# Attention-to-sampling hand-over of a hybrid decoder step: order of the absorption's transpositions, two-half weight return, later sigmoids, gate products in the last head pair

## The reference, cut to what matters

```python
o_a = _prompt_attention(q, keys, vals) * jax.nn.silu(z_a)        # 16 heads of 64, blocks of 128 queries
...
q_lat = jnp.einsum('bthd,rhd->bthr', q[..., :QK_NOPE] * g_k[:QK_NOPE], w_uk)   # the absorption
...
s = (jnp.einsum('thr,kr->htk', ql, c_all) + jnp.einsum('thr,kr->htk', qp, kp_all))
...
o_a_s = _sample_attention(...) * jax.nn.silu(z_a_s)
```

## Time and profile before

| | us |
|---|---|
| median of 3 runs | 1684.92 |
| lowest and highest | 1684.82, 1685.46 |
| the profiled execution, its own time | 1686.57 |
| its span, first to last instruction | 1684.9 |
| PE busy | 1617.1 (96%) |
| DVE, ACT, POOL busy | 728.8 (43%), 569.8 (34%), 132.2 (8%) |

### The profile page before, as it was taken

How to read it: one execution, slowest core, us unless ns; L and a number is a source line. 1 busy time by engine, 2 the same in 40 slices (tenths; PEclk the granted TensorE clock), 3 DMA queues, 4 the chain that set the end, 5 groups by cost and what they waited for, 6 DMA issues and landing times.

```text
span 1684.9 us, 35416 instructions
## 1 busy us (share of the span) xinstructions
PE 1617.1 (96%) x14350; PEld 1196.4 (71%) x14350; DVE 728.8 (43%) x1578; ACT 569.8 (34%) x1370; POOL 132.2 (8%) x235
## 2 busy tenths in 40 slices
PE   6999999999999999978999999999999999999998
PEld 4555666688888888756777777677767777777753
DVE  3243544446444444336566565666566422000011
ACT  3155444434333333133544535343444220000000
POOL 0000321400222221020000000000000000000000
PEclk9999999969999999998999999999999989999999
DMA  9623788503444443320111111111111326323001
GB/s 330 240 81 117 218 229 275 138 7 104 117 118 118 117 113 96 88 56 18 44 36 39 47 42 48 29 46 49 40 34 40 106 81 222 82 50 85 14 25 56
DMA packets 179400, 159.87 MB, mean 95 GB/s; under 512 B 37754, under 2 KB 157562, under 8 KB 178220
## 3 DMA queue, kind: packets, MB, share of 16 engines
q1 hardware_dynamic: 168668, 118.46, 25.0%
q0 software_dynamic: 9648, 36.19, 7.2%
q10 hardware_dynamic: 928, 3.05, 0.5%
HBM read 133.02 MB, written 24.64 MB: 94 GB/s over the span
## 4 chain that ended last, share of the span: by engine, by line
PE 41%; issue 6%; ACT 4%; DVE 4%; DVEq 2%; POOLq 0%; POOL 0%; ACTq 0%
PE me_bank L2643 11%; PE rw_bank L1570 10%; PE me_bank L2653 3%; PE me_bank L2603 2%; DVE rw_gram L2313 2%; PE rw_bank L1654 1%; PE rw_bank L1725 1%; PE rw_bank L1673 1%; PE rw_bank L1584 1%; ACT rw_XF L2036 1%; PE rw_bank L1802 1%; PE rw_bank L1750 1%; DVE rw_X L2320 1%; DVEq L2314 1%; PE rw_bank L1555 1%
## 5 line engine op out<-in xcount | busy, mean ns | idle before, releaser
L1570 PE MATMUL rw_bank<-hT,big 128*128 128x288 f32 x768 | 209.3, 419 | 1.1 <-DVE prep L2288 1.0
L1570 PEld LDWEIGHTS rw_bank<-hT,big 128*128 128x128 f32 x768 | 141.3, 191 | 40.2 <-issue 3.7
L1111 PE MATMUL sa_psS<-qlT,sa_cT_pages 128*128 128x128 f32 x1024 | 133.0, 284 | 0.0
L1111 PEld LDWEIGHTS sa_psS<-qlT,sa_cT_pages 128*128 128x128 f32 x1024 | 120.7, 194 | 7.8 <-issue 0.2
L1206 ACT COPY sa_cT_pages<-sa_psA 128x512 f32<-128x512 f32 x128 | 68.7, 589 | 155.0 <-PE sa_psA L1096 155.0
L1251 DVE TENSOR_TENSOR sa_ST<-sa_psS,kinvp 128x512 f32<-128x512 f32 x64 | 44.2, 691 | 154.0 <-PE sa_psS L1111 153.4
L2708 DVE TENSOR_TENSOR big<-me_bank,prep 128x288 f32<-128x288 f32 x24 | 9.9, 452 | 170.2 <-PE me_bank L2643 170.2
L1584 PE MATMUL rw_bank<-hT,big 128*128 128x288 f32 x256 | 73.5, 421 | 0.0
L739 PE MATMUL pr_psZ<-hT,qlT 128*128 128x288 f32 x256 | 72.8, 406 | 0.0
L2675 ACT ACTIVATE prep<-me_bank 128x288 f32<-128x288 f32 x12 | 4.9, 410 | 185.8 <-PE me_bank L2643 185.8
L853 ACT ACTIVATE pr_pb<-pr_psS,pr_nmx,qs 128x128 f32<-128x128 f32 (+3 forms) x64 | 39.5, 617 | 78.6 <-PE pr_psT L748 46.2
(11 more groups left out here) (499 smaller groups left out, 3137.7 us busy)
## 6 DMA issues: line engine op xcount, KB each, us to landing
big<-in_w_in SPq DMA_DIRECT2D x42, 512.0 KB, 4.2
big<-in_cache_kv POOLq DMA_DIRECT2D x80, 128.0 KB, 3.2
pages<-in_cache_kv POOLq DMA_DIRECT2D x80, 128.0 KB, 2.7
fr_wada<-in_w_ada SPq DMA_DIRECT2D x8, 1024.0 KB, 11.6
qk_scratch<-oaT SPq DMA_DIRECT2D x32, 192.0 KB, 2.5
big<-in_cache_kv SPq DMA_DIRECT2D x48, 128.0 KB, 2.7
pages<-in_cache_kv SPq DMA_DIRECT2D x48, 128.0 KB, 2.8
fr_wada<-in_w_ada SPq DMA_DIRECT2D x2, 2048.0 KB, 10.5
```

Source lines behind the costliest of these rows:

```text
L1111: last = nc.tensor.matmul(psS[:, c, 0:ROW], cT[:, g % 2, r, c * P:(c + 1) * P], M.qlT[:, r, n, :, :].rearrange("p h t -> p (h t)"), start= ...
L1570: last = mm(bank[h][:, 0:HT], w[:, ORDER[q], k, :], M.hT[:, k, (F0, F1)[h]], start=(k == 0), stop=(k == KT - 1))
```

## The change

Four edits:

1. `gates`: the last pair takes 10 pieces in its units instead of 12, as 1, 1, 1, 1, 1, 2, 2, 1. The 2 that are left stand after the last unit, ahead of the last `values`.
2. `absorb` on PE: the 8 transpositions of w_uk for k = 0 come first (banks 0 and 1) and increment `tr`; then the 8 for k = 1 (banks 2 and 3), `tr` again; then the 8 of the queries. The wait for the z copies stands only before these. The rope key gives the third increment.
3. The transposed half k = 0 is copied by DVE after the first increment and half k = 1 by ACT after the second, each over its own half of w_uk, laid out as rank half, head pair, rank. A new semaphore `uk_sb` marks DVE's copies. `sample` on PE waits first for `uk_sb`, and the products wait for `tr_sb` (the query copy) as well as for ACT's copies. The copies of the rope key and of the queries wait for the third increment, and so does SP's load of the own-token mask.
4. The first two sigmoids of the prompt's gates, with their table load, go from ahead of ACT's copies to behind ACT's first key and latent copies in `sample`.

```diff
-        in_pair = lambda hp: (0, 3, 3, 2, 2, 2, 2, 2) if hp == 0 else (2, 2, 2, 2, 1, 2, 1, 2 if hp + 1 < NP else 0)
+        in_pair = lambda hp: (0, 3, 3, 2, 2, 2, 2, 2) if hp == 0 else (2, 2, 2, 2, 1, 2, 1, 2) if hp + 1 < NP else (1, 1, 1, 1, 1, 2, 2, 1)
...
                 if u < ALL:
                     gates(range(begun[u], begun[u + 1]))
+                else:
+                    gates(range(begun[u], 2 * KT * NP))
...
+            for e in range(begun[ALL] // KT, 2 * NP):
+                gates_to_sbuf(e)
...
-        ukT = M.wuk[:, :, :].rearrange("p a n -> p (a n)").rearrange("p (h r) -> p h r", r=KL)
+        ukT = M.wuk[:, :, :]
...
             if rt == 0:
+                pe.wait_ge(uk_sb, 1)
                 pe.wait_ge(tr_sb, 1)
...
+            pe.wait_ge(M.wuk_in, 16)
+            for k in range(2):
+                for hp in range(NP):
+                    last = nc.tensor.transpose(bank[2 * k + hp // 4][:, (hp % 4) * P:(hp % 4 + 1) * P], M.wuk[:, k, hp * P:(hp + 1) * P], M.ident[:, :])
+                last.then_inc(tr, 1)
             pe.wait_ge(M.zraw_sb, 2 * NP)
-            pe.wait_ge(M.wuk_in, 16)
             for hp in range(NP):
-                for k in range(2):
-                    nc.tensor.transpose(bank[hp // 2][:, (hp % 2) * KL + k * P:(hp % 2) * KL + (k + 1) * P],
-                                        M.wuk[:, k, hp * P:(hp + 1) * P], M.ident[:, :])
                 nc.tensor.transpose(bank[6][:, hp * SB:(hp + 1) * SB],
...
+            act.wait_ge(tr, 2)
+            for n in range(2):
+                last = nc.scalar.copy(ukT[:, 1, 512 * n:512 * n + 512], bank[2 + n][:, :])
+            last.then_inc(act_sb, 1)
             act.wait_ge(M.pv, PB * NP)
-            gate_sigmoid(act, 0)
-            gate_sigmoid(act, 1)
-            act.wait_ge(tr, 1)
-            for n in range(2, 4):
-                last = nc.scalar.copy(ukT[:, 2 * n:2 * n + 2, :], bank[n][:, :].rearrange("p (a r) -> p a r", r=KL))
-            last.then_inc(act_sb, 1)
...
             for n in range(2):
-                v.tensor_copy(ukT[:, 2 * n:2 * n + 2, :], bank[n][:, :].rearrange("p (a r) -> p a r", r=KL))
+                last = v.tensor_copy(ukT[:, 0, 512 * n:512 * n + 512], bank[n][:, :])
+            last.then_inc(uk_sb, 1)
             dve.drain()
+            dve.wait_ge(tr, 3)
...
-            pe.wait_ge(M.absorb_tr_sb, 1)
+            pe.wait_ge(M.uk_sb, 1)
             key_transposes(0)
...
             latents_to_sbuf(0, 0)
+            M.gate_sigmoid(act, 0)
+            M.gate_sigmoid(act, 1)
```

More of the change, by code:

```diff
@@ L890, in absorb @@
         tr, tr_sb, mm, ev, act_sb, sigmoids, silus, gated = (sem(n) for n in ("tr", "tr_sb", "mm", "ev", "act_sb", "sigmoids", "silus", "gated"))
+        uk_sb = sem("uk_sb")
         block = M.block
@@ L898, in products @@
                 b = 64 * (h % 2)
-                last = nc.tensor.matmul(product_banks[rt][h % 2][:, (h // 2) * SB:(h // 2 + 1) * SB], ukT[b:b + 64, h // 2, rt * P:(rt + 1) * P],
+                last = nc.tensor.matmul(product_banks[rt][h % 2][:, (h // 2) * SB:(h // 2 + 1) * SB], ukT[b:b + 64, rt, (h // 2) * P:(h // 2 + 1) * P],
                                         qgT[b:b + 64, h // 2, :], start=True, stop=True)
@@ L916, in absorb @@
         M.absorb_products, M.gate_sigmoid, M.gate_prompt = products, gate_sigmoid, gate
-        M.absorb_tr, M.absorb_tr_sb, M.absorb_ev, M.gated = tr, tr_sb, ev, gated
+        M.absorb_tr, M.uk_sb, M.absorb_ev, M.gated = tr, uk_sb, ev, gated
         @block.tensor
@@ L1044, in _ @@
         def _(sp):
-            sp.wait_ge(M.absorb_tr, 1)
+            sp.wait_ge(M.absorb_tr, 3)
             sp.dma_start(own, I["own_mask"]).then_inc(own_in, 16)
```

## The result

| | before | after |
|---|---|---|
| median | 1684.87 us (4 runs, 1684.4 to 1685.46) | 1670.92 us (4 runs, 1670.86 to 1672.88) |
| ratio | | 0.992, 95% interval 0.9903 to 0.9937 |
| profiled execution, own time and span | 1686.57, 1684.9 | 1670.86, 1669.2 |
| mean granted clock | 0.981 | 0.989 |

A forecast was written before the change was run, and what follows sets the result against it. PE, busy 96% of the span, was taken as the bound, at half clock through most of the absorption. Terms of -1.05, -3.1, -1.0 and -0.55 summed to -5.7 us, from 1684.92 to 1679.2 us; range 1674 to 1684.5.

The forecast's parts named there:

- term 1: Last pair's gate pieces (edit 1): the clock no longer falls at 337, absorption starts at 340.65, -1.05 us.
- term 2: Transpositions of w_uk and queries ordered by kind (edit 2): the block takes 2.8 us in place of 5.86, -3.1 us.
- term 3: Halves and signals (edit 3), rope key to key transpositions: 1.6 us in place of 2.58, no wait left, -1.0 us.
- term 4: Clock's return behind the first score product: 1.1 us less at half speed, saving -0.55 us.
- Rival D: Clock stays full through the absorption: 7.5 us more, less about 1 for copies, -12.2, 1672.7 us; chance 0.10.
- the five: The prediction's five outcomes: 1679.2, 1681.9, 1683.9, 1672.7 and 1688.9 us, with chances 0.50, 0.20, 0.10, 0.10 and 0.10.

The follow-up runs named there:

- kinds_only: Kernel before with the queries' transpositions in a loop of their own behind those of w_uk, still one signal: ratio 0.9971, median 1678.5 us.
- mixed_kinds: Changed kernel with the queries' transpositions put among those of w_uk's second half: ratio 0.9958, median 1675.33 us.
- gates_only: Kernel before with edit 1 (the last pair's gate pieces) alone: ratio 1.0007, median 1682.32 us.
- gates_again: Kernel before with edit 1 alone, profiled once more: 1683.11 us.
- kinds_again: Kernel before with the queries' transpositions in their own loop behind those of w_uk, profiled once more: 1678.59 us.
- twice_transposed: Changed kernel with each transposition of w_uk done twice, 32 in place of 16: ratio 0.9962, median 1676.7 us.
- after_again: Changed kernel, unchanged, run once more on a later chip: ratio 0.9945, median 1673.19 us against 1683.54.
- before_again: Kernel before, unchanged, profiled once more: 1676.89 us.
- order_only: Changed kernel with the last pair's gate pieces as before (edits 2, 3 and 4 without 1): ratio 0.9945, median 1671.43 us.
- order_again: Edits 2, 3 and 4 without edit 1, profiled once more: 1671.87 us.

## Why the prediction was wrong

**The arrival, term 1: right in number, in part by luck.** -1.05 was forecast, and 341.71 - 340.65 = -1.06 measured in the first pair of profiles. The 0.28 us of the first unit came (from 315.93 to 320.72 it was 4.79 us, from 316.19 to 320.71 4.52), the wait at 334.83 filled to 0.41, and the clock held at 337. But the execution of after was already 316.19 - 315.93 = 0.26 late ahead of the first edited piece, so the edit was worth 1.33 there. And nearly all of it is the clock's: in seven of the nine profiles without edit 1 nothing fell at 337, and there the edit is worth 0.1 us.

**The block, term 2: right, small error.** 340.65 to 343.09 is 2.44 us against 2.8 forecast, so -3.4; the eight small transpositions took 0.55. Measured at the full clock on both sides, kinds_only against before gives 15.9 - 13.9 = 2.0, and that is what the order saves when no clock is lost. There are 14 changes of kind fewer, 0.15 us each. (Two bounds of this term are a tenth off: 5.17 - 5.86 is -0.7, and 2.36 - 5.86 is -3.5.)

**The signals, term 3: right in kind.** 344.23 - 343.09 = 1.14 us against 1.6 forecast, so 2.58 - 1.14 gives -1.4 for -1.0. At the full clock the signals are worth 13.9 - 12.5 = 1.35 us, about the wait of 1.27 for DVE. I had read that wait as 0.56, because in that profile PE was at half speed and arrived late.

**The step that failed** is the sentence "The rest to the first score product at 363.80 is the same PE work at half speed", together with the half clock from 343.9 that I took over from one profile. The work from the key transpositions to the score product took 363.80 - 350.15 = 13.65 us before and 352.08 - 344.23 = 7.85 after, 5.8 us that no term had. The scores behind it ran at full speed as well: from there to the third group's transpositions it was 370.86 - 363.80 = 7.06 us, and 357.40 - 352.08 = 5.32 after, so the return of the clock gave 1.74 in place of term 4's 0.55. Rival D had the first of these, as 7.5 us less 1 for copies, with a chance of 0.10; its 1672.7 us is the nearest of the five. At 357.40 the changed kernel is 13.46 us ahead.

**Why it failed.** I reckoned the half clock of one profile as certain on both sides of the change. For the kernel before it was nearly so: 51 of its 52 timed executions have a mean clock like that of the profiles with a loss. For the changed kernel it was not: 43 of the 44 executions with its order and signals have 0.987 or more, and none of their 8 profiles lost the clock behind 340.5. The change takes away two things, the mixture and the wait of 1.27 us, and the counts between say that each matters by itself. With the wait alone (kinds_only) 7 of 10 executions have the low mean, and with half of the mixture alone (mixed_kinds) 5 of 10. The falls were seen right after the wait (gates_only, gates_again, kinds_again) and in the mixed transpositions (before, mixed_kinds). What in them makes the clock fall in one execution and not in another stays open.

**Transpositions and the clock.** The prediction leaned on the Trainium skill, TensorE: Matmul & The Clock Gate, Part 4, that transposes don't count as busy for the gate in the way of matmuls, and said that the dense block wouldn't hold the clock. In twice_transposed PE did almost nothing but transpositions from 340.6 to 347, and the clock stayed full. The measurement decides against that use of the rule here: in these rows it is changes of kind and waits around the transpositions that go with a loss, not transpositions as such. The prediction's row for the rule was weak as well: of the 3.3 us from 340.5 to 343.8 the first 1.2 were the end of `values` and the spreading product, up to 341.71.

**The sum.** Work alone is 2.0 + 1.35 + 0.1 = 3.5 us, and a clock kept in the absorption another 23.2 - 15.9 = 7.3 us in an execution that would have lost it as the first profile did, and 1.7 more under the first scores. In the first pair of profiles before had lost it, and edit 1 gave 1.33 in place of 0.1: 2.04 + 1.35 + 1.33 + 7.26 + 1.74 = 13.72 us, less the 0.26 by which the execution of after was late before the change, 13.46, as measured at 357.40. In the comparison of after_again the medians are 10.4 us apart (1683.54 and 1673.19), between the two. There the losses may have been smaller: gates_only and gates_again, also mixed and with one signal, lost 5.2 and 5.8 us and not 7.3.

**What stays open.** Why two of the three profiles of before kept the clock when 1 of its 52 timed executions looks like it, and why the first comparison gave 14 us and the later one 10.4. Between the profile of before_again and that of after 6.0 us remain, of which the stage explains 3.4. The RWKV stage, which the change doesn't touch, took 706.1 us in the one and 700.9 in the other (703.1 in the first profile of before), from its first transposition to the merge's first product of `hT` and `me_w` (L2643 of before). That length differs between executions of one kernel: order_only had 700.9 and order_again, the same kernel, 704.6. The stage from 1337 still shows half speed (0.57 over 7 us in the windows above). This too isn't fixed by the kernel: it was about 10 us of half speed in gates_only and 7 in gates_again. No version ran faster than the changed kernel by more than the intervals.

## What to carry to other kernels

Ahead of a forecast that hangs on the granted clock, profile the kernel before more than once and look at the mean clock of its timed executions. A fall in one picture is a chance, its price enters the sum multiplied by it, and the changed kernel has a chance of its own. At a hand-over between stages, group TensorE's small instructions by shape, and signal each part as it is complete, so that no copy on another engine stands between two blocks: here that was worth 3.4 us as work, and 4.5 to 7.3 us more where it kept a clock that would have been lost. Before moving an instruction out of a gap, ask what the gap covers: with both products together a wait of 0.41 us became one of 1.25.

## What the runs showed of the hardware

- TensorE kept its full clock over a block of 32 transpositions of 128x128 in 3.64 us (0.11 us each), with eight of 64 rows, sixteen more and eight key transpositions behind it.
- 14 changes fewer between 128-row and 64-row transpositions shortened the block by 2.0 us at the full clock (15.9 in before_again, 13.9 in kinds_only), 0.15 us each. At half clock the weight loads sat idle 0.33 us ahead of each 64-row one that followed a 128-row one.
- The executions of before lay between 1676.9 and 1690 us, but for one; in its three profiles the stretch around the change took 15.9, 15.9 and 23.2 us with the same instructions, at the full clock and at half.
- The table load of ACT and the two sigmoids behind it took 350.71 + 1.26 - 349.41 = 2.56 us in `sample`, with 0.02 us between the load and the first sigmoid, and no drain beside them showed, as in the earlier trace rows.
